# First MoE: three weight transfers of 4 MB per expert in place of six of 2 MB

## The chip, the cores and the metric

The kernel runs on one core of a Trainium2 chip. The metric is device time in microseconds of one execution. A core has TensorE (matrix products into PSUM), VectorE, ScalarE, GpSimd and SyncE; here SyncE does nothing but wait and issue the weight transfers, and sixteen DMA engines carry each transfer from HBM to SBUF.

## The reference

Two transformer blocks, one after the other, on 256 tokens of width 1024, all in float32. Each block has a token mixer and a mixture of experts. The part that is changed is the first block's mixture:

```python
def moe_ffn(h, w_router, b_router, w_up, b_up, w_down, b_down):
    ...
    def expert_block(args):
        xb, e = args
        hu = xb @ w_up[e] + b_up[e]
        x_glu = jnp.minimum(hu[:, ::2], SWIGLU_LIMIT)
        x_lin = jnp.clip(hu[:, 1::2], -SWIGLU_LIMIT, SWIGLU_LIMIT)
        act = x_glu * jax.nn.sigmoid(SWIGLU_ALPHA * x_glu) * (x_lin + 1.0)
        return act @ w_down[e] + b_down[e]
    ...
```

There are 32 experts. `w_up[e]` is 1024 x 2048 (8 MB) and `w_down[e]` 1024 x 1024 (4 MB), so an expert's weights are 12 MB, and all of them are read whatever the router says. The second block has a mixture of 32 smaller experts, taken four at a time.

## The kernel before

Weights stream through a ring of six slots of 2 MB (16 KB in each of 128 partitions): slots 0 to 3 lie side by side in `ring4`, slots 4 and 5 in `ring2`. The kernel numbers its 2 MB loads as units; `SLOT_OF` gives a unit's slot, `loaded(u)` the semaphore and count that say that it has landed, and `unit_free(u)` the semaphore and count that say that TensorE is done with it.

An expert of the first MoE is six units: units 0 to 3 are quarters of `w_up` (slots 2, 3, 4, 5), units 4 and 5 are halves of `w_down` (slots 0, 1). The ring holds exactly one expert. TensorE's work on an expert is `moe1_pe`: four groups of matmuls, one for each up unit, and each ends with an increment of `m1_up_done`; then the gather of the next expert's tokens and the scatter of the last expert's result; a wait for the activation, which VectorE and ScalarE work out after the fourth up unit; some transposes; then two groups of matmuls for the down units, and each ends with an increment of `m1_down_done`. Each group waits for its own unit first (`arrived(pe, i)`).

SyncE issues all weight loads in one fixed order. L737 to L739 issue the first expert's six units, each when the slot's earlier content is used up. Then a loop over experts 1 to 31 (L742 to L748) waits, for each unit, until TensorE has used the same unit of the expert before, and issues the load. After the loop come the loads for the second block's projections (`unit_load`, L205), the first of them into slot 0, when the last expert's unit 4 is used.

A float32 matmul of the program stands in the trace as two records, so that the 8 matmuls of a unit are 16 records there.

Of the kernel before, what the change touches and what calls it, by code (L numbers as in the profile page):

```python
# [67 lines left out]
for _n, _w in [("w_r1", KD * NE), ("w_r2", KD * 36), ("hg_gain", 128), ("q_gain", 64), ("k_gain", 64), ("sink", 8),  # L68
# [12 lines left out]
             q=(0, 4), k=(4, 4), b=(8, 4), v=(12, 4), tmp=(16, 4), reset=(16, 4), qt=(20, 4), oT=(20, 4), vv=(24, 1),  # L81
# [14 lines left out]
MOE1 = len(PRE)  # L96
MID0 = MOE1 + 6 * NE
MID = [("in", i) for i in range(10)] + [("cv",), ("sb",), ("out", 0), ("out", 1)]
MOE2 = MID0 + len(MID)
# [7 lines left out]
def program(nc, t, out):  # L107
    ctx = ExitStack()
    with ctx:
# [5 lines left out]
        def S(name):  # L115
            if name not in sems:
                sems[name] = ctx.enter_context(nc.semaphore(name))
            return sems[name]
# [60 lines left out]
        def before_in_slot(u):  # L179

            return max(v for v in range(u) if SLOT_OF[v] == SLOT_OF[u])

        def unit_load(eng, u, desc, done=None):
# [20 lines left out]
                src = w[0, :, desc[1] * 512:(desc[1] + 1) * 512].rearrange("(k p) n -> p k n", p=P)  # L204
            eng.dma_start(dst, src).then_inc(done or S(f"loaded{s}"), 16)  # L205

        def loaded(u):

            return S(f"loaded{SLOT_OF[u]}"), 16 * SLOT_OF[:u + 1].count(SLOT_OF[u])

        def big_rounds():

# [13 lines left out]
        def unit_free(u):  # L226

            if u < MOE1 and PRE[u][0] == "ada":
                return S("ada_done"), ADA.index(u) + 1
            if MOE1 <= u < MID0:  # L230
                i = (u - MOE1) % 6
                e = (u - MOE1) // 6
                return (S("m1_up_done"), 4 * e + i + 1) if i < 4 else (S("m1_down_done"), 2 * e + i - 3)
            return S("big_done"), [n for n, r in enumerate(ROUNDS) if r[0] == u and r[3]][0] + 1
# [9 lines left out]
        def wait(eng, sv):  # L244
            eng.wait_ge(sv[0], sv[1])
# [58 lines left out]
        def moe1_src(e, i):  # L304
            w = w_up_u if i < 4 else w_dn_u
            j = i if i < 4 else i - 4
            return w[bass.ds(e, 1), j, :, :, :].rearrange("o p k n -> p (o k) n")

        def moe1_dst(i):
            return slots[SLOT_OF[MOE1 + i]].rearrange("p (k n) -> p k n", k=2 if i < 4 else 4)  # L310

        def moe2_src(quad, i):
            w = t[("w_gate_e_2", "w_up_e_2", "w_down_e_2")[i // 2]][0]
            return w[bass.ds(4 * quad + 2 * (i % 2), 2), :, :].rearrange("o (p k) n -> p o (k n)", p=P)
# [15 lines left out]
        def quad_loaded(q, i, register=None):  # L330

            s_ = quad_slot(q, i)
            n = SLOT_OF[:MOE2].count(s_) + sum(1 for p in range(q + 1) if s_ in (QUAD0, QUAD1, LATER)[min(p, 2)])
            if register is None:
                return S(f"loaded{s_}"), 16 * n
            return S(f"loaded{s_}"), 16 * register + 16 * (n - q)
# [393 lines left out]
        def _(sp):  # L730
# [3 lines left out]
                    wait(sp, unit_free(before_in_slot(u)))  # L734
                unit_load(sp, u, d)

            for i in range(6):  # L737
                wait(sp, unit_free(before_in_slot(MOE1 + i)))
                sp.dma_start(moe1_dst(i), moe1_src(0, i)).then_inc(S(f"loaded{SLOT_OF[MOE1 + i]}"), 16)  # L739
            sp.wait_ge(S("m1_flag"), 1)  # L740
            more = sp.value_load(flag[0:1, 0:1], min_val=0, max_val=SEQ)
            with sp.Fori(1, NE) as e:  # L742
                for i in range(6):
                    if i < 4:
                        sp.wait_ge(S("m1_up_done"), 4 * e + (i - 3))
                    else:
                        sp.wait_ge(S("m1_down_done"), 2 * e + (i - 5))
                    sp.dma_start(moe1_dst(i), moe1_src(e, i)).then_inc(S(f"loaded{SLOT_OF[MOE1 + i]}"), 16)  # L748

            for n in range(4):  # L750
                wait(sp, unit_free(before_in_slot(MID0 + n)))
# [296 lines left out]
        def _(pe):  # L1048
# [283 lines left out]

            def arrival(e):
                def arrived(pe, i):
                    sl, n = loaded(MOE1 + i)
                    pe.wait_ge(sl, 16 * e + n)
                return arrived

            moe1_pe(pe, "m1", 0, 0, arrival(0), True, False, bias_rows)
# [772 lines left out]
```

## Time and profile before

| | us |
|---|---|
| median of three runs | 1707.29 (1705.9 to 1708.4) |
| profiled execution, its time | 1712.5 |
| profiled execution, its span | 1710.7 |
| TensorE busy in the span | 1542.8 (90%) |
| VectorE busy | 575.5 (34%) |
| ScalarE busy | 273.4 (16%) |

The first MoE runs from about 328 us to about 1260 us of the span, which is more than half of it. The profile's page gives the chain of work that ended last: DMA holds 48% of it and TensorE 45%. The page's strip in 40 slices (43 us each) shows where the transfers run without a break. A row of a timeline or chain gives the start, the duration, the engine and line, and what was done; brackets hold the idle time before it and what ended that.

### The profile page before, as it was taken

The page shows a single profiled execution, that of the slowest core. Times are in us where ns is not written, and L with a number is a line of the kernel's source. Part 1 is how long each engine was busy: PE and PEld are TensorE (multiplying, and loading weights), DVE is VectorE, ACT ScalarE, POOL GpSimd, SP SyncE. Part 2 cuts the span into 40 slices and gives each one's busy share as a digit, 9 for nine tenths or more (in the row PEclk, how much of TensorE's full clock was granted, in tenths as well). Part 3 has the DMA queues.
Part 4 walks back from the last instruction along what each step waited for, and adds up shares of the span by engine and source line. Part 5 has one row for each costly group of instructions (what it writes and reads, how often), then busy time and mean ns, then how long its engine had stood idle before and what let it go on. Part 6 is the DMA issues. An engine that isn't in the chain of part 4 may idle for free.

```text
span 1710.7 us, 20294 instructions
## 1 busy us (share of the span) xinstructions
PE 1542.8 (90%) x8314; PEld 768.3 (45%) x8314; DVE 575.5 (34%) x1051; ACT 273.4 (16%) x345; POOL 11.9 (1%) x24
## 2 busy tenths in 40 slices
PE   3999999999999898999999898989979999997677
PEld 1656875433333232333333232323338898653343
DVE  2382133331323131313222231313156586431211
ACT  2040010110101010101011110101023464111010
POOL 1000000000000000000000000000000000000000
PEclk9999899999999999999999999999989999999889
DMA  9956234299999999999999999999974446699996
GB/s 347 375 224 258 100 126 160 96 406 428 429 428 428 428 429 429 429 428 428 429 429 428 428 429 428 429 429 429 428 297 150 146 148 248 256 395 421 422 422 280
DMA packets 73232, 592.26 MB, mean 346 GB/s; under 512 B 4946, under 2 KB 6056, under 8 KB 33252
## 3 DMA queue, kind: packets, MB, share of 16 engines
q1 hardware_dynamic: 71856, 588.27, 83.4%
q0 software_dynamic: 1088, 2.74, 0.7%
q8 instruction: 34, 0.56, 0.1%
q10 hardware_dynamic: 244, 0.61, 0.1%
q14 instruction: 10, 0.08, 0.0%
HBM read 590.55 MB, written 1.05 MB: 346 GB/s over the span
## 4 chain that ended last, share of the span: by engine, by line
DMA 48%; PE 45%; DVE 5%; issue 1%; ACT 1%; SPq 0%; DVEq 0%; ACTq 0%
PE PS L451 40%; DMA ring<-in_w_up 39%; DMA ring<-in_w_up_e 6%; PE PS L589 3%; DMA ring<-in_w_ada 2%; DMA ring<-in_w_down_e 1%; PE PS L611 1%; PE PS L1134 1%; DVE ring_r L297 1%; PE PS L541 0%; DVE arena L1887 0%; ACT ring_r L292 0%; DVE arena L678 0%; DVE arena L1958 0%; ACT hT L901 0%
## 5 line engine op out<-in xcount | busy, mean ns | idle before, releaser
L451 PE MATMUL PS<-ring,arena 128*64 128x512 f32 (+1 forms) x3136 | 713.1, 596 | 66.9 <-DMA ring<-in_w_up 57.5
L451 PEld LDWEIGHTS PS<-ring,arena 128*64 128x64 f32 (+1 forms) x3136 | 224.4, 138 | 518.4 <-issue 400.0
L451 PE MATMUL PS<-arena 64*128 64x512 f32 (+12 forms) x1176 | 228.1, 445 | 4.4 <-DVE arena L1938 1.0
L666 DVE TENSOR_SCALAR arena<-PS 128x512 f32<-128x512 f32 x32 | 22.1, 692 | 514.4 <-PE PS L451 514.4
L451 PEld LDWEIGHTS PS<-arena 128*64 128x64 f32 (+6 forms) x1176 | 115.1, 169 | 116.2 <-issue 107.3
L431 ACT ACTIVATE arena<-arena 128x512 f32<-128x512 f32 x32 | 20.2, 630 | 724.7 <-DVE arena L666 724.7
L451 PE MATMUL PS<-ring_r 128*128 128x256 f32 (+1 forms) x320 | 98.9, 309 | 0.0
L589 PE MATMUL PS<-ring,arena 128*32 128x256 f32 x928 | 66.2, 440 | 31.9 <-DMA ring<-in_w_up_e 22.7
L451 PE MATMUL PS<-hT,ring 128*128 128x256 f32 x384 | 89.9, 398 | 0.0
L451 PE MATMUL PS<-hT_r,ring_r 128*128 128x256 f32 x448 | 82.8, 286 | 1.0 <-DVE ring_r L297 1.0
L451 PEld LDWEIGHTS PS<-hT,ring 128*128 128x128 f32 x384 | 76.5, 201 | 12.5 <-issue 1.2
L297 DVE TENSOR_TENSOR ring_r<-ring,ring_r 128x2048 fp32r<-128x2048 f32 x28 | 63.7, 2290 | 34.0 <-ACT ring_r L292 33.6
L451 PEld LDWEIGHTS PS<-hT_r,ring_r 128*128 128x128 f32 x448 | 71.0, 194 | 1.4 <-DVE ring_r L297 1.2
L660 DVE TENSOR_TENSOR x<-x,PS 128x2048 f32<-128x2048 f32 x31 | 70.6, 2279 | 0.0
L292 ACT ACTIVATE ring_r<-ring 128x2048 fp32r<-128x2048 f32 x28 | 53.4, 1910 | 82.7 <-PE PS L451 68.1
L451 PEld LDWEIGHTS PS<-ring_r 128*128 128x128 f32 x320 | 62.4, 195 | 2.7
L589 PEld LDWEIGHTS PS<-ring,arena 128*32 128x32 f32 x928 | 34.5, 126 | 60.4 <-DMA ring<-in_w_up_e 24.2
L690 DVE TENSOR_TENSOR arena<-PS,arena 128x512 f32<-128x512 f32 x32 | 22.1, 691 | 112.4 <-PE PS L451 112.4
L451 PE MATMUL PS<-ring_r,hT_r 128*128 128x512 f32 x160 | 52.0, 404 | 4.6 <-issue 3.1
L451 PE MATMUL PS<-ring,hT 128*128 128x512 f32 (+1 forms) x128 | 52.2, 567 | 3.6 <-ACT hT L901 3.6
L451 PE MATMUL PS<-consts 128*128 128x512 f32 x82 | 42.8, 673 | 4.8 <-issue 4.3
L611 PE MATMUL PS<-ring,arena 128*32 128x512 f32 x256 | 30.8, 622 | 11.0 <-DMA ring<-in_w_down_e 7.0
(364 smaller groups left out, 1096.9 us busy)
## 6 DMA issues: line engine op xcount, KB each, us to landing
ring<-in_w_up SPq DMA_DIRECT2D x128, 2048.0 KB, 25.2
ring<-in_w_down SPq DMA_DIRECT2D x64, 2048.0 KB, 21.7
ring<-in_w_in SPq DMA_DIRECT2D x19, 2048.0 KB, 8.0
ring<-in_w_down_e SPq DMA_DIRECT2D x16, 2048.0 KB, 20.4
ring<-in_w_up_e SPq DMA_DIRECT2D x15, 2048.0 KB, 19.6
ring<-in_w_gate_e SPq DMA_DIRECT2D x14, 2048.0 KB, 19.6
ring<-in_w_ada SPq DMA_DIRECT2D x12, 2048.0 KB, 18.3
ring<-in_w_out SPq DMA_DIRECT2D x4, 2048.0 KB, 7.9
```

Source lines behind the costliest of these rows:

```text
L292: nc.scalar.activation(upper(n), PIECES[n][2], ACT.Copy).then_inc(S("w_upper"), 1)
L297: nc.vector.tensor_tensor(w_r, w, upper(n), ALU.subtract).then_inc(S("w_lower"), 1)
L431: nc.scalar.activation(sg, glu, ACT.Sigmoid, scale=1.702).then_inc(S(f"{X}_sg"), 1)
L451: return nc.tensor.matmul(o, w, m, start=first, stop=last)
L589: mm_ = nc.tensor.matmul(PS[q, 2 + i, 0:256], xg2[:, k * P + CAP2 * j:k * P + CAP2 * (j + 1)], moe2_dst(where, 2 * i + j // 2)[:, 8 * (j % ...
L611: mm_ = nc.tensor.matmul(PS[q, b, :], aT2[:, kk * P + CAP2 * j:kk * P + CAP2 * (j + 1)], moe2_dst(where, 4 + j // 2)[:, 2 * (j % 2) + kk, ...
L660: V.tensor_tensor(xflat, xflat, PS[:, 4:8, :].rearrange("p b n -> p (b n)"), ALU.add).then_inc(S(f"{X}_added"), 1)
L666: V.tensor_scalar(glu.rearrange("p (kk b q) -> p kk b q", kk=4, b=2), hu[:, :, :, :, 0], 7.0, None, ALU.min)\
L690: V.tensor_tensor(ye[:, 0:512], PS[:, 1, :], g2h, ALU.mult).then_inc(S(f"{X}_ye"), 1)
L1134: last = nc.tensor.matmul(PS[32 * j:32 * j + 32, 7 if b != 1 else 6, :], sm("cond32")[:, 32 * k:32 * k + 32], w[:, kk, 512 * j:512 * (j + 1)],
```

## The change

The six transfers of an expert become three: units 0 and 1, units 2 and 3, units 4 and 5. Each goes into two neighbouring slots by one issue. SyncE waits until both slots are free before it issues. TensorE waits before units 0, 2 and 4 only, for the pair; the waits before units 1, 3 and 5 are gone. A pair increments the semaphore of its first slot alone, and the counting functions (`loads_into`, `loaded`, `quad_loaded`) follow that. The matmuls, their order and the increments of `m1_up_done` and `m1_down_done` stay as they are. The loop for overfull experts (L757 to L761), which is entered only when an expert has more than 64 tokens, keeps its six transfers.

```diff
+        def second_of_pair(u):
+            return MOE1 <= u < MID0 and (u - MOE1) % 2 == 1
+
+        def loads_into(s_, end):
+            return sum(1 for v in range(end) if SLOT_OF[v] == s_ and not second_of_pair(v))
+
         def loaded(u):
-            return S(f"loaded{SLOT_OF[u]}"), 16 * SLOT_OF[:u + 1].count(SLOT_OF[u])
+            if second_of_pair(u):
+                return loaded(u - 1)
+            return S(f"loaded{SLOT_OF[u]}"), 16 * loads_into(SLOT_OF[u], u + 1)
...
+        def moe1_pair_src(e, i):
+            w = w_up_u if i < 4 else w_dn_u
+            j = i if i < 4 else 0
+            return w[bass.ds(e, 1), j:j + 2, :, :, :].rearrange("o i p k n -> p (o i) (k n)")
+
+        def moe1_pair_dst(i):
+            s_ = SLOT_OF[MOE1 + i]
+            ring = ring4[:, s_:s_ + 2, :] if s_ < 4 else ring2[:, :, :]
+            return ring
...
-            for i in range(6):
+            for i in range(0, 6, 2):
                 wait(sp, unit_free(before_in_slot(MOE1 + i)))
-                sp.dma_start(moe1_dst(i), moe1_src(0, i)).then_inc(S(f"loaded{SLOT_OF[MOE1 + i]}"), 16)
+                wait(sp, unit_free(before_in_slot(MOE1 + i + 1)))
+                sp.dma_start(moe1_pair_dst(i), moe1_pair_src(0, i)).then_inc(S(f"loaded{SLOT_OF[MOE1 + i]}"), 16)
...
             with sp.Fori(1, NE) as e:
-                for i in range(6):
+                for i in range(0, 6, 2):
                     if i < 4:
-                        sp.wait_ge(S("m1_up_done"), 4 * e + (i - 3))
+                        sp.wait_ge(S("m1_up_done"), 4 * e + (i - 2))
                     else:
-                        sp.wait_ge(S("m1_down_done"), 2 * e + (i - 5))
-                    sp.dma_start(moe1_dst(i), moe1_src(e, i)).then_inc(S(f"loaded{SLOT_OF[MOE1 + i]}"), 16)
+                        sp.wait_ge(S("m1_down_done"), 2 * e)
+                    sp.dma_start(moe1_pair_dst(i), moe1_pair_src(e, i)).then_inc(S(f"loaded{SLOT_OF[MOE1 + i]}"), 16)
...
             def arrival(e):
                 def arrived(pe, i):
-                    sl, n = loaded(MOE1 + i)
-                    pe.wait_ge(sl, 16 * e + n)
+                    if i % 2 == 0:
+                        sl, n = loaded(MOE1 + i)
+                        pe.wait_ge(sl, 16 * e + n)
                 return arrived
```

On SyncE, the loop over experts 1 to 31 stood like this before. `m1_up_done` and `m1_down_done` are the counts that TensorE raises after each unit's matmuls, and 128x4096 is the shape written, 16 KB for each partition:

```order
L742 UNCONDITIONAL_BRANCH
L742 ISA
L748 ISA [waits m1_up_done]
L748 DMA ring<-in_w_up 128x4096
L745 REGISTER_ALU
L748 ISA [waits m1_up_done]
L748 DMA ring<-in_w_up 128x4096
...
L747 ISA
L748 ISA [waits m1_down_done]
L748 DMA ring<-in_w_down 128x4096
L748 ISA [waits m1_down_done]
L748 DMA ring<-in_w_down 128x4096
```

And the same loop now:

```order
L763 UNCONDITIONAL_BRANCH
L763 ISA
L769 ISA [waits m1_up_done]
L769 DMA ring<-in_w_up 128x2x4096
L769 ISA [waits m1_up_done]
L769 DMA ring<-in_w_up 128x2x4096
L768 REGISTER_ALU
L769 ISA [waits m1_down_done]
L769 DMA ring<-in_w_down 128x2x4096
```

Six pairs of wait and issue have become three. Each issue writes two rows of 16 KB for each partition, and no load has been moved past another.

On TensorE, an expert inside the loop stood like this before, from its first up unit to its second down unit (`loaded2` is the semaphore of slot 2, and so on; `arena` holds the tokens and activations):

```order
L451 MATMUL PS<-ring,arena 64x512 [waits loaded2]
L451 MATMUL PS<-ring,arena 64x512 x7
L451 MATMUL PS<-ring,arena 64x512 [waits loaded3]
L451 MATMUL PS<-ring,arena 64x512 x7
L451 MATMUL PS<-ring,arena 64x512 [waits loaded4]
L451 MATMUL PS<-ring,arena 64x512 x7
L451 MATMUL PS<-ring,arena 64x512 [waits loaded5]
L451 MATMUL PS<-ring,arena 64x512 x7
...
L451 MATMUL PS<-ring,arena 64x512 [waits loaded0]
L451 MATMUL PS<-ring,arena 64x512 x7
L451 MATMUL PS<-ring,arena 64x512 [waits loaded1]
L451 MATMUL PS<-ring,arena 64x512 x7
```

And now:

```order
L471 MATMUL PS<-ring,arena 64x512 [waits loaded2]
L471 MATMUL PS<-ring,arena 64x512 x15
L471 MATMUL PS<-ring,arena 64x512 [waits loaded4]
L471 MATMUL PS<-ring,arena 64x512 x15
...
L471 MATMUL PS<-ring,arena 64x512 [waits loaded0,m1_aT]
L471 MATMUL PS<-ring,arena 64x512 x15
```

The matmuls are the same 48 in the same order; the waits for slots 3, 5 and 1 are gone, and unit 2's matmuls now wait for the transfer that brings unit 3 too.

## Rows read from the trace of the kernel before

**Rows 1.** The page: 40 slices of the span, and the chain's shares.

```profile
DMA  9956234299999999999999999999974446699996
GB/s 347 375 224 258 100 126 160 96 406 428 429 428 428 428 429 429 429 428 428 429 429 428 428 429 428 429 429 429 428 297 150 146 148 248 256 395 421 422 422 280
...
DMA 48%; PE 45%; DVE 5%; issue 1%; ACT 1%; SPq 0%; DVEq 0%; ACTq 0%
```

**Rows 2.** The chain in order of time: start, duration, what; PE-led, then DMA-led.

```profile
380.68 25.27 PE PS L451 x114
407.39 25.27 PE PS L451 x114
434.11 25.27 PE PS L451 x114
...
482.63 24.94 DMA ring<-in_w_up
507.62 3.68 PE PS L451 x16
...
1186.98 25.49 DMA ring<-in_w_up
1212.52 3.68 PE PS L451 x16
```

**Rows 3.** Timeline, start of the first MoE: first expert and the first refills.

```profile
331.92 13.95 PE L451 MATMUL PS<-ring,arena 128*64 128x512 f32 x64 [0.69 <-ACT arena L426]
335.77 10.61 SPq L748 DMA_DIRECT2D ring<-in_w_up  x4
353.63 7.42 PE L451 MATMUL PS<-ring,arena 128*64 128x512 f32 x32
357.80 3.77 SPq L748 DMA_DIRECT2D ring<-in_w_down  x2
361.64 13.95 PE L451 MATMUL PS<-ring,arena 128*64 128x512 f32 x64
365.48 10.63 SPq L748 DMA_DIRECT2D ring<-in_w_up  x4
...
384.51 3.77 SPq L748 DMA_DIRECT2D ring<-in_w_down  x2
```

**Rows 4.** Timeline, the last expert and the first load after the MoE.

```profile
1228.93 3.65 PE L451 MATMUL PS<-ring,arena 128*64 128x512 f32 x16
1232.95 3.65 PE L451 MATMUL PS<-ring,arena 128*64 128x512 f32 x16 [0.36 <-DMA ring<-in_w_up]
1237.68 3.65 PE L451 MATMUL PS<-ring,arena 128*64 128x512 f32 x16 [1.08 <-DMA ring<-in_w_up]
1242.58 3.65 PE L451 MATMUL PS<-ring,arena 128*64 128x512 f32 x16 [1.24 <-DMA ring<-in_w_up]
1250.58 7.09 PE L451 MATMUL PS<-ring,arena 128*64 128x512 f32 x32 [0.57 <-DVE arena L678]
1254.28 36.84 SPq L205 DMA_DIRECT2D ring<-in_w_in  x5
```

**Rows 5.** Packets by size and total, in 600:1200, then in 1575:1685, then in 1262:1274.

```profile
DMA packets 17647, 257.12 MB, mean 429 GB/s; under 512 B 1954, under 2 KB 1954, under 8 KB 1954
DMA packets 6013, 46.39 MB, mean 422 GB/s; under 512 B 351, under 2 KB 351, under 8 KB 351
DMA packets 2272, 4.63 MB, mean 386 GB/s; under 512 B 32, under 2 KB 32, under 8 KB 2268
```

**Rows 6.** Issues in 600:1200: what, count, size, median us to landing.

```profile
ring<-in_w_up SPq DMA_DIRECT2D x80, 2048.0 KB, 25.4
ring<-in_w_down SPq DMA_DIRECT2D x42, 2048.0 KB, 22.4
```

**Rows 7.** The chain in the second MoE: start, duration, what.

```profile
1602.22 23.94 DMA ring<-in_w_up_e
1626.20 6.02 PE PS L589 x64
1632.71 23.27 DMA ring<-in_w_up_e
1656.02 6.41 PE PS L589 x64
```

**Rows 8.** Timeline, SyncE's loads of the first expert.

```profile
215.45 0.34 SPq L739 DMA_DIRECT2D ring<-in_w_up  x1
...
291.51 0.33 SPq L739 DMA_DIRECT2D ring<-in_w_down  x1
305.25 0.33 SPq L739 DMA_DIRECT2D ring<-in_w_down  x1
```

**Rows 9.** Line 739, issue to landing: min, median, max.

```profile
DMA to landing us min/median/max: 7.6/7.6/7.8
```

**Rows 10.** Timeline, TensorE's waits for transfers in the second MoE.

```profile
1556.57 3.66 PE L589 MATMUL PS<-ring,arena 128*32 128x256 f32 x64 [2.44 <-DMA ring<-in_w_gate_e]
1667.49 3.64 PE L611 MATMUL PS<-ring,arena 128*32 128x512 f32 x32 [1.07 <-DVE arena L722]
1695.85 5.27 PE L611 MATMUL PS<-ring,arena 128*32 128x512 f32 x32 [2.65 <-DMA ring<-in_w_down_e]
```

**Rows 11.** Windows: length, busy PE, PEld, DVE, ACT, POOL, granted clock, DMA share, GB/s.

```profile
600.00:1187.30 587.30, 538.97 (x2482) 184.81 (x2480) 157.16 (x281) 62.15 (x80) 0.00 (x0) 1.00 1.01 428
1557.00:1560.00 3.00, 3.00 (x60) 1.69 (x52) 1.32 (x8) 0.00 (x0) 0.00 (x0) 1.00 1.00 418
1695.00:1698.00 3.00, 2.15 (x12) 0.68 (x16) 0.00 (x0) 0.00 (x0) 0.00 (x0) 0.63 0.00 0
```

More of the change, by code:

```diff
@@ L332, in quad_loaded @@
             s_ = quad_slot(q, i)
-            n = SLOT_OF[:MOE2].count(s_) + sum(1 for p in range(q + 1) if s_ in (QUAD0, QUAD1, LATER)[min(p, 2)])
+            n = loads_into(s_, MOE2) + sum(1 for p in range(q + 1) if s_ in (QUAD0, QUAD1, LATER)[min(p, 2)])
             if register is None:
```

## The prediction

> **What bounds the kernel now.** I read the page's strip and chain first. From slice 9 to slice 28 the DMA engines run at 428 or 429 GB/s without a break, and DMA is the largest holder of the chain [rows 1]. So in the first MoE the question is the stream of weights, and TensorE only where the stream starts and ends.
>
> The chain in order of time shows two regimes [rows 2]. Up to 482 us it is TensorE's: experts start at 380.68, 407.39 and 434.11, one per 26.71 us. From 482 us it alternates between 25.5 us of a transfer and 3.68 us of TensorE, and the period is (1212.52 - 507.62) / 24 = 29.37 us per expert (24 periods lie between the two rows). That is six transfers of 4.895 us. The 25.5 us are not slowness: a transfer waits behind about four others that are queued, as the 25.4 us from issue to landing say [rows 6]; an issue into an empty queue lands in 7.6 us [rows 9]. So TensorE frees slots long before the stream needs them, and has 29.37 - 26.71 = 2.66 us per expert to spare, which it idles before units 1, 2 and 3 (0.36, 1.08 and 1.24 us; the last expert's rows show the same three) [rows 4].
>
> A stream that never breaks has a simple end: its start, plus its content times its rate. What TensorE does in between drops out. The change can therefore act in four places: when the unbroken stream starts, how long a megabyte takes, whether the stream breaks, and what TensorE still has to do after the transfer that it waits for last.
>
> **The start of the stream.** The first expert's weights are loaded long before they are used. The first refill is issued at 335.77, when unit 0 of the first expert is used; the four up issues take 10.61 us from first to last, so units are used (10.61 - 0.33) / 3 = 3.43 us apart [rows 3]. Four transfers last 19.6 us, to 355.4 on the issue clock; the first down refill is issued only at 357.80, when its slot is free. There the stream breaks for about 2.4 us, and from 357.80 on it never breaks again: the second down unit is issued at 361.24, before the first is through.
>
> With pairs, the first refill waits for units 0 and 1: 339.2. The second is issued at 346.05, before the first is through. Two pairs last to 358.8. The down pair waits for both down units: 361.24. So the break stays, and the unbroken stream starts at 361.24 in place of 357.80: **+3.44 us**.
>
> Does it break later? The down pair ends at 361.24 + 9.79 = 371.0; the next up pair is issued at 365.48 + 3.43 = 368.9, 2.1 us early. The next down pair has to be issued by 371.0 + 19.6 = 390.6, and its slots are free at 384.51 + 3.44 = 387.95, 2.7 us early. From then on the stream falls behind TensorE by 29.37 - 26.71 per expert, and the margins grow until TensorE waits. There the tightest one is the down pair: it lands 9.8 us after the second up pair, and the next one starts 19.6 us later. TensorE ends the down units 6.9 us (units 2 and 3), about 4.9 us (what lies between: 26.71 less 13.95 for the up units, 7.09 for the down units and 0.7 for the bias) and 7.1 us after the second up pair has landed, 18.9 us in all; the stream needs the slots after 29.4 us less the latency of issue and landing, which is at most 7.6 - 4.9 = 2.7. The margin is 7.8 us. No break.
>
> The loads of the first expert cost nothing. The last of them is issued at 305.25 in both kernels, now with 4 MB, and lands near 305.25 + 7.6 + 4.9 = 317.8 [rows 8, 9]; its first use is at 353.63 [rows 3].
>
> **The rate.** Both kernels move rows of 16 KB. The window 600:1200 has 17647 packets, of which 1954 are under 512 B; the rest is 16.4 KB each, and 1954 is 16 for each of the 122 transfers issued there, so each DMA engine closes a transfer with one tiny packet [rows 5, 6]. The new transfers have the same rows (128x2x4096, 16 KB each) and half as many closing packets. What is one worth? Three streams without a break give the cost of a packet: 4.895 us per 2 MB with 8 packets per engine; in the second MoE (1656.02 - 1626.20) / 6 = 4.97 us with 16 packets of 8 KB [rows 7, 5]; and 2.097 MB / 386 GB/s = 5.43 us with 64 packets of 2 KB [rows 5]. The slopes agree: 0.075 / 8 = 9.4 ns and 0.535 / 56 = 9.6 ns per packet and engine. I take a closing packet as a packet like any other, 0.010 us. From the unbroken start on there are 91 pairs, each with one closing packet less: **-0.9 us**. The bounds: 0 if it overlaps the data; from above, the nearest row is the whole gap between the 16 KB and the 8 KB stream, 0.075 us, which would be 91 x 0.075 = -6.8 us.
>
> The Trainium skill, DMA: Bandwidth & Descriptors, section "Anatomy of one DMA", gives a fixed cost near 2.0 us and bytes over 436 GB/s per DMA, and calls the semaphore's write essentially free. Here the 2 us do not show when transfers queue: 4.895 us each, where that sum would be 6.8 us. By its bandwidth alone 2 MB last 4.81 us and leave 0.085 us per transfer for everything else; if all of it went with the transfer, dropping 91 would give 7.7 us, and by the rule of the free semaphore 0.
>
> The new transfer alternates between two regions 2 MB apart. The second MoE's loads alternate too (two expert matrices in one load), and their rate lies on the packets' line drawn from the 2 KB stream, whose loads do not: 4.895 + 8 x 0.0096 = 4.972 against 4.97. I take 0 for it. If the line were an accident and all of the 0.075 us came from alternating, it would be +182 x 0.075 = +13.7 us.
>
> **The end.** The last wait for a transfer that holds TensorE up is the one before unit 3, at 1242.58: units 4 and 5 are there in time (7.09 us for both without a break) [rows 4]. In the new kernel the same bytes land at the same point of the stream, but TensorE then has units 2 and 3 to do, not 3 alone. All behind it, the activation, the down units, the scatter and the loads of the second block, which start when unit 4 is used (1254.28), moves by one unit's matmuls. One unit is 13.95 / 4 = 3.49 us, 3.43 by the issues; I take **+3.45 us**. The stream itself ends later than unit 3's landing by 9.8 us, and TensorE reaches the down units 11.3 us after it, so the last pair is still in time. The waits and issues that are gone are worth nothing: SyncE is idle most of the time, and TensorE's waits only move.
>
> **The sum.** 3.44 + 3.45 - 0.9 = +6.0 us. The profiled execution took 1712.5 us, so its counterpart should take 1718.5. The runs had a median of 1707.29, 5.2 us below the profiled one; the difference applies to it unchanged: **1713.3 us**. Differences under 0.2% (3.4 us) can hardly be told from none here.
>
> **The rivals.**
>
> A. Dropping a closing packet is worth more than a packet. The place is each DMA engine between two transfers of the loop, the price is 91 times what one transfer's end costs, and it decides from 6.9 / 91 = 0.076 us on: above that the kernel is not slower. For it: only that the trace has no stream that differs in transfer size alone. Against it: 0.076 us is the cost of eight packets of any other kind. At its nearest row, 0.075 us, the time is 1707.29 + 6.9 - 6.8 = 1707.4. Were it twice that, 1700.6.
>
> B. The granted clock falls in the longer wait. TensorE's spare 2.66 us now come in one piece, before unit 2, where the longest was 1.24. In the second MoE a wait of 2.65 us before the last down group was followed by a granted clock of 0.63 (a mean between the levels of 2.4 and 1.2 GHz), and the group took 5.27 us where the same 32 records take 3.64: +1.63 [rows 10, 11]. But a wait of 2.44 us at 1554 left the clock at 1.00, and 64 records took their 3.66 us. In the middle of the MoE the loss hides in the next wait; only in the last expert it adds to the tail: 1713.3 + 1.6 = 1714.9. The stretch around is dense, 539 of 587 us busy at clock 1.00 [rows 11], and that stays so. The Trainium skill, TensorE: Matmul & The Clock Gate, section "HAM oscillation — how this bites in real kernels", warns of just this, a DMA wait per tile that re-throttles each tile. The trace's two rows stand on either side.
>
> C. Alternating regions slow the stream. Price and evidence as above: 1713.3 + 13.7 = 1727.0 at the far bound.
>
> D. One of the two shifts doesn't come. If the break at 355 were longer than I read it, the later start would be partly hidden in it; or the landing of a pair isn't one unit later than the first half's. Then 1713.3 - 3.4 = 1709.9.
>
> **How the numbers follow.** My forecast has 63% (its own range is 1711 to 1715.5, the scatter of the runs and 0.5 us on each term). B has 12%, C 5%, D 6%, A at about the break-even 9%, A beyond it 5%. Slower by over 0.2% (above 1710.7) are the forecast, B and C and a part of D: 81%. Within 0.2%: the rest of D and A near its row: 13%. Faster: 6%. The range leaves out C and A beyond break-even, and reaches the lower bound of the closing packet's cost: 1707.3 to 1717.5.
>
> **What the profile will show.** The chain should still be the stream's, with a period of 29.37 - 0.03 = 29.34 us per expert, and TensorE should have one wait of about 2.7 us per expert, before unit 2, at clock 1.00. The first refill should be issued near 339.2, the first down refill at 361.2 in place of 357.80. The last expert's unit 2 should start near 1242.6 + 3.4 - 0.9 = 1245.1, and its down group near 1256.6 in place of 1250.58. The loads of the second block should be issued near 1260.3. Everything after that should have before's durations. Packets under 512 B should be halved in 600:1200. I am wrong if the period moves by more than 0.1 us (3 us over the stream; the rate then was the question, not the ends), if the DMA share falls under 1.00 in the middle (a break that I ruled out), or if the second block's part changes by itself.

## The result, and the profile after

The changed kernel has a median of 1713.2 us over 20 runs (1705.47 to 1723.81); the kernel before, in 20 runs beside it, 1707.2 (1702.65 to 1710.18). The ratio is 1.0037, 95% interval 1.0023 to 1.0051, so the change costs 6.0 us, or between 3.9 and 8.7. The prediction was 1713.3. The profiled execution took 1714.38 us, with a span of 1712.6.

The page's strip and chain of the changed kernel, which answer to [rows 1]:

```profile
DMA  9956332499999999999999999999974446699997
GB/s 347 383 193 257 124 126 111 162 388 429 429 429 428 428 429 429 429 429 429 428 429 429 429 429 429 429 428 428 427 288 148 148 148 258 246 373 422 422 422 300
...
PE 47%; DMA 45%; DVE 5%; issue 1%; ACT 1%; SPq 0%; POOL 0%; DVEq 0%; ACTq 0%
```

The stream is as full as before and as fast. Its packets in 600:1200, and the issues there (what, count, size, median us to landing), against [rows 5, 6]:

```profile
DMA packets 16667, 257.09 MB, mean 428 GB/s; under 512 B 976, under 2 KB 976, under 8 KB 976
...
ring<-in_w_up SPq DMA_DIRECT2D x41, 4096.0 KB, 21.8
```

The closing packets are halved (976 for 1954), the bytes are the same. The chain in order of time (start, duration, what) answers to [rows 2]:

```profile
419.59 7.11 PE PS L471 x32
426.85 22.06 DMA ring<-in_w_up
448.95 7.11 PE PS L471 x32
456.21 22.06 DMA ring<-in_w_up
478.32 8.81 PE PS L471 x32
487.28 20.37 DMA ring<-in_w_up
...
1183.30 7.11 PE PS L471 x32
1190.56 22.06 DMA ring<-in_w_up
1212.66 8.81 PE PS L471 x32
1221.62 21.69 DMA ring<-in_w_up
1243.35 8.81 PE PS L471 x32
```

Two things stand here. The period is (1212.66 - 419.59) / 27 = 29.373 us, against 29.371 before: nothing came of the smaller number of transfers. And a group of 32 records, the two units behind TensorE's one wait, takes 7.11 us in 17 of the 29 experts that wait, and 8.6 to 8.8 in the other 12. The timeline of the start answers to [rows 3]:

```profile
334.80 7.23 SPq L769 DMA_DIRECT2D ring<-in_w_up  x2
349.83 8.52 PE L471 MATMUL PS<-ring,arena 128*64 128x512 f32 x32
358.53 0.37 SPq L769 DMA_DIRECT2D ring<-in_w_down  x1
358.94 13.96 PE L471 MATMUL PS<-ring,arena 128*64 128x512 f32 x64
366.20 7.24 SPq L769 DMA_DIRECT2D ring<-in_w_up  x2
```

and that of the end to [rows 4]:

```profile
1234.21 7.09 PE L471 MATMUL PS<-ring,arena 128*64 128x512 f32 x32
1243.35 8.78 PE L471 MATMUL PS<-ring,arena 128*64 128x512 f32 x32 [2.05 <-DMA ring<-in_w_up]
...
1260.18 34.07 SPq L205 DMA_DIRECT2D ring<-in_w_in  x5
```

Positions in two profiles can't be compared as they stand: the stretch before the MoE was 4.4 us shorter in this profile than in that of before (the first up matmul at 327.52 against 331.92), the stretch after it 4.0 us shorter (452.42 against 456.42). Both are code that the change doesn't touch, and both wander from profile to profile: over the twelve profiles whose MoE is compared here the first lasts 324.95 to 333.13 us and the second 451.0 to 458.6, in no order that follows the change. So I cut the first MoE out of each profile, into three parts: **head**, from the first expert's first up matmul to the first down issue (before: 357.80 - 331.92 = 25.88); **stream**, from there to the end of TensorE's last wait for weights (1242.58 - 357.80 = 884.78); **tail**, from there to the first issue of the next weights (1254.28 - 1242.58 = 11.70). The kernels that can be cut in this way, each worked out from its own timelines (four more runs, whose ends or whose stream are of another form, are told below):

| | head | stream | tail | sum | runs' median | ratio to before (95%) |
|---|---|---|---|---|---|---|
| before | 25.88 | 884.78 | 11.70 | 922.36 | 1707.2 | 1 |
| changed | 31.01 | 884.82 | 16.83 | 932.66 | 1713.2 | 1.0037 (1.0023 to 1.0051) |
| changed, again | 29.31 | 884.83 | 16.46 | 930.60 | 1713.49 | 1.0032 (1.0016 to 1.0048) |
| late issues alone | 29.32 | 884.86 | 11.70 | 925.88 | 1710.25 | 1.0009 (0.999 to 1.0027) |
| pair waits alone | 25.89 | 885.15 | 15.13 | 926.17 | 1710.48 | 1.0022 (1.0006 to 1.0039) |
| both, 2 MB transfers | 29.31 | 884.98 | 18.05 | 932.34 | 1715.36 | 1.0049 (1.0032 to 1.0067) |
| filled waits | 27.93 | 885.40 | 15.14 | 928.47 | 1710.81 | 1.0017 (1.0004 to 1.003) |
| rows of 32 KB (its output isn't the reference's) | 31.01 | 878.20 | 16.82 | 926.03 | 1706.22 | 0.9993 (0.9974 to 1.0011) |
| pairs for experts 3 to 29 | 25.74 | 885.64 | 11.71 | 923.09 | 1709.49 | 1.0021 (1.0005 to 1.0037) |
| the same, w_up in rows of 32 KB | 25.76 | 881.40 | 11.70 | 918.86 | 1705.28 | 0.9983 (0.9966 to 0.9999) |

A ratio compares with executions of the kernel before that were taken beside it (medians of 1706.98 to 1707.87). One execution of late issues alone took 2256.16 us at a granted clock of 0.651 and isn't counted.

Heads and tails repeat to some 0.1 us where the clock does the same (heads 25.88 and 25.89, or 29.31, 29.32 and 29.31; tails of 11.70 three times), while the runs of one kernel scatter by 10 us; the profile separates what the medians can't. Each row but the changed kernel's rests on one profile, though, and the streams of equal content differ by up to 0.9 us.

### The profile page after: what moved, and what is told of

It reads as the page before. It is cut to its first block, busy times and chain, and to the rows that moved or that the text cites. A ratio compares the mean times of both kernels' runs of the same rounds, so it can differ in the third digit from the quotient of the medians.

```text
span 1712.6 us, 19963 instructions
## 1 busy us (share of the span) xinstructions
PE 1552.1 (91%) x8314; PEld 768.3 (45%) x8314; DVE 575.8 (34%) x1051; ACT 273.4 (16%) x345; POOL 11.8 (1%) x24
## 4 chain that ended last, share of the span: by engine, by line
PE 47%; DMA 45%; DVE 5%; issue 1%; ACT 1%; SPq 0%; POOL 0%; DVEq 0%; ACTq 0%
PE PS L471 42%; DMA ring<-in_w_up 36%; DMA ring<-in_w_up_e 6%; PE PS L609 3%; DMA ring<-in_w_ada 2%; DMA ring<-in_w_down_e 1%; PE PS L1155 1%; PE PS L631 1%; DVE ring_r L307 1%; DMA arena<-in_b_up 0%; DVE arena L1909 0%; ACT ring_r L302 0%; PE PS L485 0%; DVE arena L1980 0%; ACT hT L922 0%
## 5 line engine op out<-in xcount | busy, mean ns | idle before, releaser
L471 PE MATMUL PS<-ring,arena 128*64 128x512 f32 (+1 forms) x3136 | 728.7, 610 | 61.0 <-DMA ring<-in_w_up 51.5
L471 PEld LDWEIGHTS PS<-ring,arena 128*64 128x64 f32 (+1 forms) x3136 | 231.4, 141 | 521.1 <-issue 433.2
L471 PE MATMUL PS<-hT,ring 128*128 128x256 f32 x384 | 85.7, 385 | 0.0
```

The lines of the kernel that those rows point to most:

```text
L471: return nc.tensor.matmul(o, w, m, start=first, stop=last)
```

## The experiments

**Both halves of the change, one at a time.** The changed kernel was profiled again first:

> The changed kernel once more, for a second profile. Theory (two shifts at the ends of the stream, and a clock that may fall in TensorE's one wait per expert): about 1713, and in the profile some of the last-pair groups of 32 records take 8.8 us in place of 7.1. From the start of the first expert's matmuls to the first load after the MoE: 932.7 in the first profile, 922.4 in the kernel before; if the clock falls neither in the first nor in the last expert, 929.3. Rival (the slower time comes from outside the MoE): the section is as long as before, 922.4.

Measured: 1713.49, and 11 of 29 groups longer than 8 us. Sum of the parts 930.60: head 29.31 (its first expert lost no more to the clock than that of the kernel before: the granted clock over the head is 0.94, against 0.93 before and 0.89 in the first profile), tail 16.46 with a last group of 8.41. The rival that puts the time outside the MoE falls.

Late issues alone, in the kernel before:

```diff
                     if i < 4:
-                        sp.wait_ge(S("m1_up_done"), 4 * e + (i - 3))
+                        sp.wait_ge(S("m1_up_done"), 4 * e + (i | 1) - 3)
                     else:
-                        sp.wait_ge(S("m1_down_done"), 2 * e + (i - 5))
+                        sp.wait_ge(S("m1_down_done"), 2 * e)
```

> Six transfers of 2 MB, and TensorE waits for each unit, as in the kernel before; SyncE alone issues by pairs: it issues an even unit only when the odd one is used too. Theory: the unbroken stream starts one unit later and nothing else moves: +3.4 us, 1710.6, the section from the first expert's matmuls to the first load after the MoE 925.8, period 29.37, TensorE waits before units 1, 2 and 3, no group at half clock. Rival (the wait of TensorE for a pair does it all): 1707.2, section 922.4. Rival (4 MB transfers do it): 1707.2.

Measured: the head is 29.32, 3.44 more than before, and stream and tail are those of before. The timeline's first up matmuls and first down issues give the head:

```profile
333.13 13.95 PE L451 MATMUL PS<-ring,arena 128*64 128x512 f32 x64 [0.69 <-ACT arena L426]
362.45 0.85 SPq L748 DMA_DIRECT2D ring<-in_w_down  x2
```

No group behind a wait for weights ran long. The sum is 925.88 for 925.8 expected. The runs' ratio alone couldn't tell it from nothing.

Pair waits alone, in the kernel before:

```diff
                 def arrived(pe, i):
-                    sl, n = loaded(MOE1 + i)
-                    pe.wait_ge(sl, 16 * e + n)
+                    if i % 2 == 0:
+                        for j in (i, i + 1):
+                            sl, n = loaded(MOE1 + j)
+                            pe.wait_ge(sl, 16 * e + n)
```

> Six transfers of 2 MB, issued as in the kernel before; TensorE alone waits by pairs, before units 0, 2 and 4 for both units. Theory: the stream starts and runs as before, period 29.37; TensorE has one wait of 2.4 to 2.7 us per expert; after the last wait two units stand in place of one: +3.45, and +1.7 more where the clock falls in the last wait. 1710.6 to 1712.3, section 925.8 or 927.5. Rival (the clock falls because of 4 MB transfers or by chance, not by the wait): no group of 8.8 us. Rival (all of it comes from late issues): 1707.2.

Measured: the head is that of before, the tail 15.13, 3.43 more. Here the last group was at full clock. From the chain of that kernel (start, duration, what):

```profile
473.48 7.10 PE PS L451 x32
480.73 21.98 DMA ring<-in_w_up
502.85 7.10 PE PS L451 x32
510.10 21.98 DMA ring<-in_w_up
532.21 8.80 PE PS L451 x32
...
1237.14 7.10 PE PS L451 x32
```

Groups of 8.80 us are there with transfers of 2 MB, and no group was longer at all in the kernel with late issues alone. So they come with the one long wait, not with the size of the transfer. The two shifts are separate and add up.

**The size of the transfer.** Both edits at once give the timing of pairs with six transfers of 2 MB:

> Both of the above at once with six transfers of 2 MB: the timing of pairs without a transfer of 4 MB. Theory with a free closing packet: the same as the changed kernel, 1713.2, period 29.37, section 929.3 to 932.7. Theory as predicted (a closing packet costs 0.010 us): 0.9 us above the changed kernel, its period 29.40. Rival (the size of the transfer itself costs or gives something): period unlike the changed kernel's 29.37 by over 0.03 us.

Measured: period 29.371, for 29.373 with 4 MB. The sum is 932.34; its last group took 10.01 us, the longest loss of clock of all. Three closing packets fewer per expert are worth less than 0.01 us together. My price of 0.010 each is refuted, unless alternating between two regions costs the same 0.03 us. The Trainium skill, DMA: Bandwidth & Descriptors, "Anatomy of one DMA", calls the semaphore's write essentially free, of transfers that GpSimd issues; the period agrees for these, which SyncE issues.

To settle what else a large transfer changes, each partition read 32 KB in one piece:

```diff
         def moe1_pair_src(e, i):
-            w = w_up_u if i < 4 else w_dn_u
-            j = i if i < 4 else 0
-            return w[bass.ds(e, 1), j:j + 2, :, :, :].rearrange("o i p k n -> p (o i) (k n)")
+            w = t["w_up" if i < 4 else "w_down"][0].rearrange("e (j p i k) n -> e j p i k n", p=P, i=2, k=2 if i < 4 else 4)
+            j = i // 2 if i < 4 else 0
+            return w[bass.ds(e, 1), j, :, :, :, :].rearrange("o p i k n -> p (o i) (k n)")
```

> The changed kernel with another assignment of weight rows to partitions: each partition reads 32 KB in one piece in place of two rows of 16 KB that lie 2 MB apart. The products are then taken with permuted weights, so the output isn't the reference's. Theory (neither alternating regions nor closing packets cost anything): if the packets stay at 16 KB, the period is 29.37 and the time 1713. If they become 32 KB, the packets' line (0.0096 us per packet and engine, 8 fewer per 4 MB) gives 29.37 - 3 x 0.077 = 29.14 and 1706. Rival (alternating costs what the closing packets gave, 0.03 us per expert): 29.34 at 16 KB.

Measured: the packets did become 32 KB, as the line for 600:1200 says (8898 packets, 992 of them closings, and 259.07 MB: 32.8 KB for each other packet):

```profile
DMA packets 8898, 259.07 MB, mean 432 GB/s; under 512 B 992, under 2 KB 992, under 8 KB 992
```

The stream is 878.20, 6.6 us shorter, and the period 29.14 as computed. So the line of 0.0096 us per packet and engine, drawn from packets of 2, 8 and 16 KB, holds at 32 KB too. This kernel doesn't alternate and has three closing packets per expert; were the three that it drops worth 0.010 us each, its period would be 29.11. Closings are free, then, and so is alternating, since the changed kernel, which alternates and drops the same three, has 29.373. This rests on the line: the rival in which the two costs cancel survives only if a packet saved on the way to 32 KB is worth 0.0084 us and not 0.0096.

I also tried to price the end of a transfer by having twelve of 1 MB, each of 64 partitions:

```diff
-                    sp.dma_start(moe1_dst(i), moe1_src(e, i)).then_inc(S(f"loaded{SLOT_OF[MOE1 + i]}"), 16)
+                    for q in range(2):
+                        sp.dma_start(moe1_dst(i)[64 * q:64 * (q + 1)], moe1_src(e, i)[64 * q:64 * (q + 1)]).then_inc(S(f"loaded{SLOT_OF[MOE1 + i]}"), 16)
```

> The kernel before, with each 2 MB unit of experts 1 to 31 in two transfers of 64 partitions (1 MB, rows of 16 KB as before): twelve transfers per expert. It prices the end of a transfer by itself. A closing packet as dear as any other (0.010 us per DMA engine): period 29.37 + 0.06 = 29.43. The rival that broke even (0.076 us): 29.83. Free, as the changed kernel's period of 29.37 suggests: 29.37.

Measured: 2633.83 us in its one run, a period near 59.5. It answers nothing on closings, for another cost hides them: a transfer to 64 partitions moves at half the rate. Window, its length, busy times of PE, PEld, DVE, ACT and POOL, granted clock, DMA share, GB/s:

```profile
600.00:1200.00 600.00, 379.94 (x1252) 115.12 (x1254) 78.65 (x140) 31.07 (x40) 0.00 (x0) 0.78 1.01 211
```

The engines are as busy as ever (share 1.01) at 211 GB/s.

**The clock.** Two spare matmuls fill most of TensorE's long wait in the changed kernel:

```diff
             for i in range(4):
+                if i == 2 and not first:
+                    keep_warm(2, 0)
                 arrived(pe, i)
```

> The changed kernel, and in each expert but the first TensorE does two spare 128x512 matmuls into a free PSUM bank between units 1 and 2, in the time that it waited (about 1.8 us of the 2.4). Theory (the clock falls because TensorE idles 2.4 us in one piece): the second pair's 32 records take 7.1 us in every expert, and the time is at or up to 1.7 us below the changed kernel's, 1711.5 to 1713.2. Rival (the clock falls whatever fills the wait): 8.8 us still shows up as often as before. Rival (the spare matmuls are themselves on the path in the last expert): up to +1 us.

Measured: not one long group, where the changed kernel had 12. Its timeline in the last two experts, for which the changed kernel has groups of 8.78 us:

```profile
1209.97 7.09 PE L471 MATMUL PS<-ring,arena 128*64 128x512 f32 x32 [0.51 <-DMA ring<-in_w_up]
1239.34 7.09 PE L471 MATMUL PS<-ring,arena 128*64 128x512 f32 x32 [0.53 <-DMA ring<-in_w_up]
```

The wait before a group shrank to 0.5 us. The tail is 15.14, 1.7 less than the changed kernel's, and the median 1710.81 for 1713.2 and 1713.49: the difference is of the size expected, though the intervals overlap. Of its sum of 928.47 the edit explains the tail; the head is 27.93, 1.4 less than in the second profile of the changed kernel, because the first expert, which the edit doesn't touch, happened to run it at a granted clock of 1.00. What the granted clock does is shown by four windows of the changed kernel around such a wait (window, its length, busy time of PE, granted clock, DMA share, GB/s):

```profile
1210.00:1212.00 2.00, 0.23 (x2) 1.00 0.98 418
1212.00:1214.00 2.00, 1.34 (x4) 0.73 0.98 418
1214.00:1216.00 2.00, 2.00 (x8) 0.50 1.08 459
1216.00:1218.00 2.00, 2.00 (x12) 0.92 0.98 418
```

TensorE idles 2.43 us until 1212.66. The clock is at 0.50 (1.2 GHz) throughout 1214:1216, and the means of 0.73 and 0.92 beside it put the fall at about 1212.9 and the rise at about 1216.3: the 8.8 us group. The idle time alone doesn't decide it. The changed kernel's profile has 18 waits of 2.05 to 2.45 us; after 12 of them the clock fell, after 6 it stayed at 1.00 (the next group took 7.09 us), and after the 10 short waits, of 0.73 to 0.95 us, it never fell. Which of the long waits are spared isn't shown.

**Where the grain costs, and where not.** If the cost lies at the ends, single units there and pairs between should be free:

```diff
+            singles(1)
+            with sp.Fori(2, NE - 1) as e:
+                ...
+                    sp.dma_start(moe1_pair_dst(i), moe1_pair_src(e, i)).then_inc(S(f"loaded{SLOT_OF[MOE1 + i]}"), 16)
+            singles(NE - 1)
```

> Six transfers and six waits for experts 0, 1 and 31, three transfers of 4 MB and three waits for experts 2 to 30. Theory (the cost of pairs lies at the two ends of the stream alone): the time of the kernel before, 1707.2, section 922.4, though experts in the middle still show 8.8 us groups, which cost nothing. Rival (the pairs in the middle cost something): 1710 or more.

A miss: 1712.09 (1.0027, 1.0011 to 1.0042), the sum 926.04, 3.7 us over what I expected. The timeline names both losses:

```profile
355.53 3.76 SPq L758 DMA_DIRECT2D ring<-in_w_down  x2
366.79 7.24 SPq L767 DMA_DIRECT2D ring<-in_w_up  x2
...
1212.29 8.78 PE L461 MATMUL PS<-ring,arena 128*64 128x512 f32 x32 [2.43 <-DMA ring<-in_w_up]
1226.15 7.09 PE L461 MATMUL PS<-ring,arena 128*64 128x512 f32 x32 [0.20 <-DVE arena L688]
1233.83 13.95 PE L461 MATMUL PS<-ring,arena 128*64 128x512 f32 x64
```

The two down units of expert 1 are issued at 355.53 and last to 365.3 on the issue clock; the first pair is issued only at 366.79, so the stream runs dry there for 1.5 us, one expert later than in the changed kernel. And in the last expert TensorE runs its four up units without a wait (x64): it is behind the stream, for expert 30's pair set it back by 3.45 + 1.7 us, and one expert wins back 2.66. So the singles have to begin and end one expert further in:

> As the version with pairs in the middle, but with six transfers and six waits for experts 0, 1, 2, 30 and 31. That version lost 3.7 us, and its trace says where: the pair after expert 1 was issued at 366.79, after the stream had run dry, and TensorE came into the last expert about 2.5 us late, for it wins back only 2.66 us per expert of the 3.45 + 1.7 that a pair's wait at half clock puts on it. Theory (a delay of TensorE is won back at 2.66 us per expert, and two experts do): 1707.2; from the first down issue to the last wait 884.8, from there to the next load 11.70, as in the kernel before. Rival (pairs in the middle cost something that isn't won back): 1710 or more.

Measured: head 25.74 and tail 11.71 are back to before's, the stream is 885.64, 0.9 over. By the profile the pairs in the middle cost 0.7 us, by the runs 3.6 (0.9 to 6.3). The low end of the interval agrees with the profile; the middle doesn't, and I have no mechanism for a difference outside the MoE. That stays open. For the 0.9 us in the stream there is a candidate: experts 1, 2 and 30 now have code of their own beside the loop, and between 320 and 1262 us the profile has 7 packets of 16 KB on the queue named instruction, where that of the kernel before has 3. One such packet holds one of the 16 DMA engines for about 1 us. No run tests whether this is the cause.

The grain one step further, 8 MB of up weights at a time, by waits alone:

```diff
                     if i < 4:
-                        sp.wait_ge(S("m1_up_done"), 4 * e + (i - 3))
+                        sp.wait_ge(S("m1_up_done"), 4 * e)
...
+                    for j in ({0: range(4), 4: (4, 5)}).get(i, ()):
+                        sl, n = loaded(MOE1 + j)
+                        pe.wait_ge(sl, 16 * e + n)
```

> The kernel before, 2 MB transfers, but SyncE issues the four up units of an expert only when all four are used, and TensorE waits for all four before the first; down units in pairs. The changed kernel's step, taken once more. Theory (the grain costs only at the ends as long as slots are released before the stream needs them; here they aren't): the cycle becomes 19.6 of up transfers, 2.7 to issue and land, 13.8 of up matmuls = 36.1 us per expert, 37.8 to 39.5 if TensorE's idle 9.5 us per expert puts the next matmuls at half clock; 1950 to 2010 in all. Rival (the stream stays the bound and the grain acts at the ends only): period 29.37, one more step at either end, about 1727.

Measured: 2010.23 us in one run, at the upper end of what I expected, and 38.8 us per expert. Its timeline shows the cycle: transfers, 9.7 to 10.0 us of idle TensorE, matmuls partly at half clock (16.87 and 15.70 for 13.95):

```profile
926.19 1.99 SPq L748 DMA_DIRECT2D ring<-in_w_up  x4
948.92 15.70 PE L451 MATMUL PS<-ring,arena 128*64 128x512 f32 x64 [9.96 <-DMA ring<-in_w_up]
964.79 2.00 SPq L748 DMA_DIRECT2D ring<-in_w_up  x4
```

So pairs are cheap only because their margins of 2.1, 2.7 and 7.8 us hold. The next doubling uses them up and costs 303 us, not another 7.

**Finer ends.** If a coarser grain costs at the ends, a finer one should pay there: the first refilled down unit and the last expert's unit 3 in two transfers of 1 MB each:

```diff
+            units(1, 4)
+            with sp.Fori(2, NE - 1) as e:
+                units(e)
+            units(NE - 1, 3)
...
+                    if kk == 1 and last and i == 3:
+                        arrived(pe, i, 1)
```

> The kernel before with finer ends: the first down unit that is refilled comes in two transfers of 1 MB, the first of them issued when half of the slot is used; and the last expert's unit 3 in two of 1 MB, with a wait for each half. If the ends price the granularity of a slot, halving it gives back half a unit at each: -1.7 (stream starts at 356.1 on the clock of the kernel before) and -1.7 (1.75 us of matmuls after the last wait in place of 3.5), less 0.08 for smaller rows: section 919.1, 1703.9. Rival (the stream's start is bound by something else, or units 4 and 5 of the last expert are then late): -1.7 or nothing.

Nothing gained: 1707.77 (0.9999, 0.9984 to 1.0013), the sum of the parts 922.37. The first half is issued 25.72 us after the first up matmul, where the kernel before issued the whole unit after 25.88: the first expert happened to run its down group partly at half clock (8.55 us against 7.42), which ate the head's gain, and unit 5 then came 5.15 us after the first half, more than unit 4 lasts. In the last expert the waits before units 2 and 3 merged into one. How much the finer pieces would give at full clock isn't settled by this run.

**Longer rows.** The experiments say that a 4 MB transfer buys something only if its rows get longer. In the version with single units for experts 0, 1, 2, 30 and 31, w_up's rows were assigned so that a partition reads 32 KB in one piece, and the tokens' columns were regrouped in a copy that ScalarE does anyway:

```diff
-        w_up_u = t["w_up"][0].rearrange("e (i p k) n -> e i p k n", p=P, k=2)
+        w_up_u = t["w_up"][0].rearrange("e (j p i k) n -> e j i p k n", p=P, i=2, k=2)
...
-                                 PS[:, 0, :].rearrange("p (i q k) -> p i k q", i=2, k=2), ACT.Copy)
+                                 PS[:, 0, :].rearrange("p (q i k) -> p i k q", i=2, k=2), ACT.Copy)
```

> Pairs of 4 MB for experts 3 to 29 alone, as in the version before, and w_up's rows assigned so that a partition reads 32 KB in one piece in a pair (the tokens' columns are regrouped to match in the copy that ScalarE does anyway); w_down keeps two rows of 16 KB. Theory (what a larger transfer can buy is fewer packets, at 0.0096 us each per DMA engine): 8 packets fewer in each of two pairs per expert, the period inside the loop 29.37 - 0.154 = 29.22; 27 experts give -4.2 us, on top of the version with five experts in single units, 1709.5: 1705.3, or 1703 if that version's true cost over the kernel before is the 0.8 us of its profile. Rival (packets of 32 KB gain only where all transfers have them): 29.37.

Measured: 1705.28, ratio 0.9983 (0.9966 to 0.9999); the stream is 881.40, 4.24 us under the same version with 16 KB rows, for 4.2 expected. It is the only kernel here whose interval lies below 1, and barely; one such interval among ten changed kernels is weak evidence by itself. The stronger is the profile's MoE, 918.86 for 922.36, with the shorter period that the rows foretold.

## Why the prediction was right

**The start.** +3.44 was predicted; +3.44 came with late issues alone (29.32 against 25.88) and in the second profile of the changed kernel (29.31). The first profile has 31.01. Its first expert lost 1.7 us more to a lower clock, 1.1 of it in the down group, which took 8.52 us where [rows 3] have 7.42.

**No break.** The margins held: the up pair behind the first down pair was issued 7.67 us after it (366.20 against 358.53), 2.1 us before that was through. The stream is 884.82 and 884.83 for 884.78, the DMA share 1.01 in the middle.

**The rate.** This step was wrong. I took a closing packet for a packet like any other and subtracted 0.9 us; it is worth nothing that the period shows (29.373 for 29.371, where I had 29.34). The slope itself was right and foretold the 32 KB rows to 0.01 us; what failed was to count the closing among the packets that the slope is about. The rival that dropping it is worth a break-even 0.076 us (14% together) falls with it, and so does C: alternating slowed nothing that the period shows.

**The end.** +3.45 was predicted; +3.43 came with pair waits alone (15.13 against 11.70). With both halves of the change the tails were 16.83, 16.46 and 18.05: the rest is the last group at a lower clock, +1.7, +1.3 and +2.9. Neither shift stayed away, as D had it.

**The clock.** I gave it 12% as a rival, and it was the normal case: the clock fell after 12 and 11 of 29 waits, and after the last wait of both profiles. I had set one row of a wait that kept the clock against one that didn't, and let the dense work around decide for it. Neither row decides it: 12 and 11 of the 18 long waits lost the clock, the others kept it. It was right that this costs nothing in the middle: after a long group the next wait is 0.7 us in place of 2.4, and the period stays.

**The sum.** The point came out within 0.1 us of the median, and that is luck. My two errors don't cancel: the -0.9 that wasn't there and the loss of clock in the last wait, about +1.5, which I had left to a rival, both made the forecast too low. With both set right the sum is 3.44 + 3.45 + 1.5 = 8.4 us, which is what the second profile has (8.2; the first has 10.3, with 1.7 more in the head). The runs' 6.0 is less than the parts add up to, and it is this gap that the errors happened to match. The 8.2 is inside the runs' 3.9 to 8.7, so the two don't contradict each other. Late issues and pair waits alone sum to 3.5 + 3.8 = 7.3 by their profiles, and 3.1 + 3.4 = 6.5 by their medians. Which of the two is nearer the truth can't be told from runs that scatter by 10 us.

**The signs in the profile.** The down group at 1256.49 and the second block's first load at 1260.18 lie within 0.1 us of the 1256.6 and 1260.3 that I gave, by luck too: this profile's MoE began 4.4 us earlier than the one that I counted from. Of my three signs of being wrong the period and the DMA share didn't show. The third, a second block that changes by itself, can't be read from a single profile: from the tail's end to the end of the span took 452.42 and 458.64 us in the two profiles of the changed kernel, and 456.42 in that of the kernel before.

## What to carry to other kernels

When a stream of transfers is the bound and doesn't run dry, the number of slots that are released and awaited together matters in two places: the first slot's release and the last wait. There the price was the work on one slot, 3.4 us each. In between, what counts is whether every slot is released before the stream comes round to it; work that margin out for each slot, for beyond it a coarser grain costs a multiple of what it did inside. Fewer transfers bought nothing here, where they queue; longer rows did. And ask whether gathering several short waits into one long one costs clock in the last of them, where nothing hides it.

## What the runs showed of the hardware

- The cost of a packet is linear and small: 0.0094 to 0.0096 us per packet and engine from 2 KB to 32 KB rows. Closing packets aren't on that line: three fewer per expert changed the period by 0.002 us.
- Transfers to 64 of the 128 partitions ran at 211 GB/s, those to all 128 at 428, with the DMA engines equally busy.
- Waits of 2.05 to 2.45 us amid dense matmuls were followed by a granted clock of 0.50 for a while in 12 of 18 cases of the changed kernel's first profile, at 1.7 us or less each; in the other 6 the clock stayed. Waits of 1.24 us, as in the kernel before, were never followed by it, nor was a wait filled down to 0.5 us.
- A lower clock isn't always behind a wait: from 345.00 to 353.60 us of the kernel before, in the first expert, TensorE was busy throughout and the granted clock was 0.84.
- The last transfer that TensorE waits for came 0.2 to 1.5 us later than the period says in seven profiles (30.69 us after the one before it in place of 29.37 in the changed kernel, 30.06 in the kernel before), but not with filled waits (29.37). This is no cost of the change: the stream lasts 884.8 to 885.0 us in five of these profiles, whether the last transfer is 0.5 or 1.3 us late, and 885.4 with filled waits. No run tells why. Each of these profiles, that with filled waits too, has one 16 KB packet of the queue named instruction between 1180 and 1262 us and none from 560 to 1180.
